# Expert choice in 44 steps a half, all 32 gate groups beside up tiles 95 to 126, and ScalarE's up program as straight code

## What is computed

```python
q = (h @ peer_q).reshape(B, S, 8, 2, 128)
scores = jnp.einsum('bshpd,hpkd->bshpk', q, peer_keys)      # 128 keys each
s, i = lax.top_k(scores, 16)
cand_s = s[..., 0, :, None] + s[..., 1, None, :]            # 256 a head
cand_i = i[..., 0, :, None] * 128 + i[..., 1, None, :]
top_s, sel = lax.top_k(cand_s, 16)
idx = jnp.take_along_axis(cand_i, sel, axis=-1)             # of 16384 experts
gate = jax.nn.softmax(top_s, axis=-1)
act = gelu(einsum('td,ted->te', h, peer_u[idx]))            # exact Gelu
out = einsum('te,ted->td', gate * act, peer_v[idx])
```

## Time and profile before

| What | us |
|---|---|
| runs: median of 3 (lowest, highest) | 4202.78 (4199.14, 4202.87) |
| the profiled execution, its own time | 4196.4 |
| its span, first to last instruction | 4194.6 |
| TensorE matmul busy in the span | 4031.4 |
| VectorE busy | 3057.9 |
| ScalarE busy | 2412.3 |
| GpSimd busy | 434.2 |

### The profile page before, as it was taken

How to read it: one execution, slowest core, us unless ns; L and a number is a source line. 1 busy time by engine, 2 the same in 40 slices (tenths; PEclk the granted TensorE clock), 3 DMA queues, 4 the chain that set the end, 5 groups by cost and what they waited for, 6 DMA issues and landing times.

```text
span 4194.6 us, 82991 instructions
## 1 busy us (share of the span) xinstructions
PE 4031.4 (96%) x30146; PEld 3719.3 (89%) x30146; DVE 3057.9 (73%) x4990; ACT 2412.3 (58%) x4061; POOL 434.2 (10%) x442
## 2 busy tenths in 40 slices
PE   6899999999999999999998999999998999999999
PEld 6899999788899999978888999988887799998887
DVE  6758879767565786986766678788775578787555
ACT  4246668544533665854556566774444466686544
POOL 0000015100000000520000000441000000052000
PEclk9999999999999999999998999999998899999999
DMA  8345442778513445367853445338883244533554
GB/s 292 108 137 178 177 172 100 246 245 289 174 48 136 168 177 180 111 211 249 284 179 106 179 175 180 143 126 298 283 288 111 82 166 178 180 131 116 193 192 155
DMA packets 203667, 749.27 MB, mean 179 GB/s; under 512 B 22704, under 2 KB 23856, under 8 KB 202192
## 3 DMA queue, kind: packets, MB, share of 16 engines
q1 hardware_dynamic: 178416, 646.51, 44.1%
q0 software_dynamic: 25056, 100.15, 7.5%
HBM read 745.52 MB, written 1.05 MB: 178 GB/s over the span
## 4 chain that ended last, share of the span: by engine, by line
PE 89%; ACT 5%; DVE 4%; issue 1%; DMA 1%; SPq 0%; ACTq 0%; DVEq 0%
PE ps L1953 15%; PE ps L1954 14%; PE ps L1960 14%; PE ps L2397 11%; PE ps L2400 11%; PE ps L2404 11%; PE ps L2379 4%; PE ps L2101 2%; ACT oh L1028 1%; ACT t_hi L656 1%; ACT oh L1020 1%; PE ps L1974 1%; DMA raw<-w_tiles 1%; PE ps L2354 1%; PE ps L2245 1%
## 5 line engine op out<-in xcount | busy, mean ns | idle before, releaser
L1129 DVE TENSOR_TENSOR t_lo<-raw,t_hi 128x1024 fp32r<-128x1024 f32 x1180 | 1445.4, 1225 | 921.8 <-ACT t_hi L656 902.3
L656 ACT CAST t_hi<-raw 128x1024 fp32r<-128x1024 f32 x1180 | 1239.5, 1051 | 1429.7 <-PE ps L2404 700.4
L1953 PE MATMUL ps<-h_hi,t_hi 128*128 128x256 f32 x5344 | 1353.3, 290 | 44.4 <-DVE h_lo L1261 20.2
L1954 PE MATMUL ps<-h_lo,t_hi 128*128 128x256 f32 x5344 | 1323.8, 285 | 0.0
L1953 PEld LDWEIGHTS ps<-h_hi,t_hi 128*128 128x128 f32 x5344 | 1031.6, 193 | 69.2 <-issue 46.0
L1954 PEld LDWEIGHTS ps<-h_lo,t_hi 128*128 128x128 f32 x5344 | 1034.8, 194 | 0.7 <-issue 0.5
L1960 PE MATMUL ps<-h_hi,t_lo 128*128 128x256 f32 x5240 | 735.1, 283 | 0.0
L1960 PEld LDWEIGHTS ps<-h_hi,t_lo 128*128 128x128 f32 x5240 | 676.1, 192 | 0.0
L2397 PE MATMUL ps<-t_hi,h_hi 128*128 128x512 f32 x2048 | 549.9, 390 | 11.6 <-DVE h_lo L1844 11.6
L2400 PE MATMUL ps<-t_hi,h_lo 128*128 128x512 f32 x2048 | 549.9, 390 | 0.0
L2404 PE MATMUL ps<-t_lo,h_hi 128*128 128x512 f32 x2048 | 548.1, 389 | 0.0
(11 more groups left out here) (291 smaller groups left out, 3413.1 us busy)
## 6 DMA issues: line engine op xcount, KB each, us to landing
raw<-u_tiles SPq DMA_DIRECT2D x512, 512.0 KB, 3.2
raw<-v_tiles SPq DMA_DIRECT2D x512, 512.0 KB, 4.2
raw<-w_tiles SPq DMA_DIRECT2D x188, 512.0 KB, 3.6
oh<-w_tiles POOLq DMA_DIRECT2D x160, 512.0 KB, 4.9
arena<-w_tiles SPq DMA_DIRECT2D x16, 512.0 KB, 3.6
arena<-keys_t POOLq DMA_DIRECT2D x4, 1024.0 KB, 5.1
arena<-mla_w POOLq DMA_DIRECT2D x1, 4096.0 KB, 14.4
arena<-lora POOLq DMA_DIRECT2D x2, 1280.0 KB, 8.1
```

The source lines that it names most:

```text
L656: act.copy(t_hi[:, j % SPL, :], raw[:, j % RAW, :]).then_inc(hi_done, 1)
L1129: tts(t_lo[:, j % SPL, :], raw[:, j % RAW, :], t_hi[:, j % SPL, :].bitcast(F32), ALU.subtract).then_inc(lo_done, 1)
L1953: mm(o, hi[:, c, :], h_hi[:, c, :], start=(c == 0), stop=False)
L1954: mm(o, hi[:, c, :], h_lo[:, c, :], start=False, stop=False)
```

## The change

The choice gets 44 steps a half: each pair of heads takes three steps (18 to 29) where it took four. The gates begin at tile LATE = 2 x 44 + 7 = 95, so all 32 groups stand beside tiles 95 to 126, with tile 127 alone behind them. GpSimd fills the slots from 95 on. The one-hot rows stay in one buffer. VectorE makes the columns and rows of group 0 behind its subtractions of tiles 92 and 93, and takes the first down tile's subtraction beside group 31, and tile 127's product last. ScalarE's part for the up tiles is a plain Python loop, so the instructions stand in a row with no branch; Exp runs between the cast and the Gelu of its tile, its table is asked for after the Gelu before, and the two passes of group 0 stand behind one Gelu each.

```diff
--- before.py
+++ after.py
@@ -131,8 +131,9 @@
 AT_TAIL, IN_NORM = 2, [0, 2, 2, 4]
 FOLDS_BEFORE = [0, 0, 48, 96, 160]
 
-RANK_KEYS, PAIRS, RANK_PAIRS, SOFT, LOOK_UP, CHOSEN = 0, 16, 18, 34, 35, 47
-STEPS = 48
+RANK_KEYS, PAIRS, RANK_PAIRS, SOFT, LOOK_UP, CHOSEN = 0, 16, 18, 30, 31, 43
+STEPS = 44
+LATE = TT * STEPS + 7
 SMALL = {"mix0": 64, "mix1": 128, "mix2": 144, "mix3": 176}
 NORMS_BEFORE = {"out0": 1, "out1": 3, "lout": 6, "wo": 8}
 HSPLIT = {"ffn0": 3, "ffn1": 6, "ffn2": 9, "ffn3": 13, "wo": 11}
@@ -337,9 +338,7 @@
         TK_SLOT = (KEYS - -(-sum(int(np.prod(shape)) for _, shape in choice) // T)) // EB * EB
         SC_SLOT = TK_SLOT - TT * 16 * P // T
 
-        assert SC_SLOT > STEPS + PAIRS + 2 and TK_SLOT > TT * STEPS + 6
-        BOTH = KEYS - TK_SLOT
-        assert BOTH < GROUPS and BOTH % 2 == 0
+        assert SC_SLOT > STEPS + PAIRS + 2 and TK_SLOT > LATE > SC_SLOT + 2 and (LATE + 1) % EB == 0 and KEYS - LATE == GROUPS + 1
         tk = carve([("w", (DC, T)), ("keys", (16, P)), ("q", (16, T)), ("gap", (SC_SLOT * T - 8192,)),
                     ("sc", (TT, 16, P)), *choice])
         sum_sb = carve([("gap", (24 * D,)), ("sum", (TT, D))])["sum"]
@@ -381,9 +380,7 @@
         wa_hi, wa_lo = h_hi, h_lo
         def hot_rows(l, m):
 
-            if m < BOTH or m % 2 == 0:
-                return acc[:, :].rearrange("p (q k) -> p q k", q=8)
-            return t_lo[:, (SEGS[f"u{l}"][0] + 1) % SPL, :].rearrange("p (q k) -> p q k", q=8)
+            return acc[:, :].rearrange("p (q k) -> p q k", q=8)
 
         hot_cols = [v[:, :, :, :].rearrange("p a q k -> p (a q) k") for v in (oh1, oh2)]
 
@@ -599,7 +596,8 @@
 
                 n = T // 8
                 pool.wait_ge(sel_ready, TT * (l + 1))
-                pool.memset(arena[:, TK_SLOT * T:KEYS * T], 1.0).then_inc(ones_in, 1)
+                pool.memset(act_slot(LATE, None), 1.0)
+                pool.memset(arena[:, (LATE + 1) * T:KEYS * T], 1.0).then_inc(ones_in, 1)
                 for m in range(n):
                     if m >= 2:
                         pool.wait_ge(gates_t, n * l + m - 1)
@@ -1033,20 +1031,19 @@
 
                 name = f"u{l}"
                 first = SEGS[name][0]
-                distances(l, 0)
-                weights(l, 0)
-                for k in range(TK_SLOT, KEYS):
+                below = SEGS[f"v{l}"][0]
+                for k in range(LATE, KEYS):
                     b = (first + k) % 2
                     if k + 2 < KEYS:
                         upper(first + k + 2, first + k + 2, None, name)
+                    elif k + 2 == KEYS:
+                        upper(below, below, None, f"v{l}")
                     else:
                         act.wait_ge(tile_used, first + k + 1)
                     act.activation(ps[:, b, 0:T], ps[:, b, 0:T], ACT.Gelu).then_inc(act_up, 1)
-                    distances(l, k - TK_SLOT + 1)
-                    weights(l, k - TK_SLOT + 1)
-                for m in range(BOTH + 1, GROUPS):
-                    distances(l, m)
-                    weights(l, m)
+                    if k - LATE + 1 < GROUPS:
+                        distances(l, k - LATE + 1)
+                        weights(l, k - LATE + 1)
 
             def peer(l):
                 project(f"q{l}", lambda k, b: act.copy(tk["q"][:, at(k), :], ps[:, b:b + 1, 0:T]), f"u{l}")
@@ -1061,23 +1058,23 @@
                 def gelu(k, i, b):
                     act.activation(act_slot(k, i), by_quads(ps[:, b, 0:T]), ACT.Gelu).then_inc(taken, 1)
 
-                def step(n, j, k, i):
-                    upper(n, j, i, name)
-                    gelu(j - first - 2, i, j % 2)
-                a = 2
-                for tt in range(TT):
-                    b = STEPS * tt + SOFT + 3
-                    in_loops(act, name, a, b, step)
-                    a = b
-                    seen(sm_in)
-                    act.activation(tk["e"][:, 2], tk["e"][:, 2], ACT.Exp).then_inc(sm_exp, 1)
-                in_loops(act, name, a, SC_SLOT + 2, step)
-                seen(ranked)
-                in_loops(act, name, SC_SLOT + 2, TK_SLOT + 2, step)
+                for k in range(2, LATE + 2):
+                    upper(first + k, first + k, None, name)
+                    if k in (SOFT + 3, STEPS + SOFT + 3):
+                        seen(sm_in)
+                        act.activation(tk["e"][:, 2], tk["e"][:, 2], ACT.Exp).then_inc(sm_exp, 1)
+                    if k == SC_SLOT + 2:
+                        seen(ranked)
+                    gelu(k - 2, None, (first + k) % 2)
+                    if k in (SOFT + 2, STEPS + SOFT + 2):
+                        act.preload_act_table(ACT.Exp)
+                    if k == LATE - 1:
+                        distances(l, 0)
+                    elif k == LATE:
+                        weights(l, 0)
                 tiles_and_hots(l)
                 name = f"v{l}"
                 first = SEGS[name][0]
-                upper(first, first, None, name)
                 act.wait_ge(gated, GROUPS * (l + 1))
 
                 def upper_gated(k, i, j):
@@ -1752,9 +1749,17 @@
                                 link(cp(idf, idx))
                             link(pair_sums(k - PAIRS))
                         elif k < SOFT:
-                            h, second = divmod(k - RANK_PAIRS, 2)
-                            link(next8(tk["c2"], cs[:, h, :], ci[:, h, :]) if second
-                                 else first8(tk["cand"][:, h, :], tk["c2"], cs[:, h, :], ci[:, h, :]))
+                            h, third = 2 * ((k - RANK_PAIRS) // 3), (k - RANK_PAIRS) % 3
+                            other = tk["cand"][:, h + 1, :]
+                            if third == 0:
+                                link(first8(tk["cand"][:, h, :], tk["c2"], cs[:, h, :], ci[:, h, :]))
+                            elif third == 1:
+                                next8(tk["c2"], cs[:, h, :], ci[:, h, :])
+                                link(dve.max(cs[:, h + 1, 0:8], other))
+                                dve.max_index(ci[:, h + 1, 0:8], cs[:, h + 1, 0:8], other)
+                            else:
+                                link(dve.match_replace(tk["c2"], cs[:, h + 1, 0:8], other, LOWEST))
+                                link(next8(tk["c2"], cs[:, h + 1, :], ci[:, h + 1, :]))
                         elif k == SOFT:
 
                             tts(e[:, 2], cs, cs[:, :, 0:1].broadcast_to([P, HEADS, TOPK]), ALU.subtract)\
@@ -1775,7 +1780,6 @@
                 for k in range(a, a + 4):
                     lower(first + k, first + k, name)
                 sel_out(1)
-                in_loops(dve, name, a + 4, TK_SLOT + 2, lambda n, j, k, i: lower(n, j, name))
 
             def gates(l):
 
@@ -1799,40 +1803,41 @@
                 def activated(k):
 
                     b = (first + k) % 2
-                    dve.wait_ge(act_up, BOTH * l + k - TK_SLOT + 1)
-                    dve.wait_ge(gated, GROUPS * l + k - TK_SLOT)
+                    dve.wait_ge(act_up, (KEYS - LATE) * l + k - LATE + 1)
+                    dve.wait_ge(gated, GROUPS * l + k - LATE)
                     tts(act_slot(k, None), by_quads(ps[:, b, 0:T]), act_slot(k, None), ALU.mult).then_inc(taken, 1)
 
                 def gate(m):
 
                     dve.wait_ge(gates_t, GROUPS * l + m + 1)
-                    dve.wait_ge(taken, TAKEN[name] + min(TK_SLOT + m + 1, KEYS))
+                    dve.wait_ge(taken, TAKEN[name] + LATE + m + 1)
                     view = act_quads[:, :, 2 * m:2 * m + 2, :].rearrange("p b q x -> p q b x")
                     bank = GATE_BANKS[m % 2]
                     tts(view, ps[:, bank:bank + 2, :].rearrange("p q (b x) -> p q b x", x=4 * EB),
                         view, ALU.mult).then_inc(gated, 1)
 
-                dve.wait_ge(sel_ready, TT * (l + 1))
-                columns(0)
-                rows(0)
+                for k in range(TT * STEPS + 4, LATE + 2):
+                    lower(first + k, first + k, name)
+                    if k == TT * STEPS + 4:
+                        dve.wait_ge(sel_ready, TT * (l + 1))
+                        columns(0)
+                    elif k == TT * STEPS + 5:
+                        rows(0)
                 dve.wait_ge(ones_in, l + 1)
-                for k in range(TK_SLOT, KEYS):
-                    m = k - TK_SLOT
-                    columns(m + 1)
+                for k in range(LATE, KEYS - 1):
+                    m = k - LATE
+                    if m + 1 < GROUPS:
+                        columns(m + 1)
                     if k + 2 < KEYS:
                         lower(first + k + 2, first + k + 2, name)
+                    else:
+                        lower(SEGS[f"v{l}"][0], SEGS[f"v{l}"][0], f"v{l}")
                     activated(k)
                     dve.wait_ge(gates_t, GROUPS * l + m + 1)
-                    rows(m + 1)
+                    if m + 1 < GROUPS:
+                        rows(m + 1)
```

(18 more changed lines are left out.)

## The result

The changed kernel takes 4136.31 us (median of 4 runs, 4135.73 to 4141.58) against 4200.96 (4 runs, 4198.74 to 4202.87): a ratio of 0.9849, 95% interval 0.9832 to 0.9866, 64.7 us less. The forecast was 4133.0, with a range of 4122 to 4150. In a later set of five rounds it was 4135.04 against 4199.03, ratio 0.9845 (0.9831 to 0.9858).

A forecast was written before the change was run, and what follows sets the result against it. TensorE, 89% of the span, was taken as the bound, so only its idle or late time counts. Savings of 4 x (12.0 + 4.2) plus 4.6 for the clock, 69.4 us, gave 4133 us, range 4122 to 4150.

The forecast's parts named there:

- Part 1: Gates moved to tiles 95 to 126, with 1.5 us idle before the down tiles: 12.0 us a layer saved.
- GpSimd's fill: Fill of the slots, grown to 8448 columns: 7.2 us, done in tile 93, before group 0 asks; cover about 4 us.
- its lead of 2.3 us: VectorE's subtractions in the up tiles run 2.3 us ahead of TensorE's need, covering middle steps of 3.05 us.
- Part 2: The choice in 44 steps a half: costed at nothing; moves 0.33 us of transposes from one stretch to the other.
- Part 3: ScalarE's up tiles written out without loops: tiles 0 to 94 take 275.5 us, 4.2 us a layer saved.
- The clock, 4.6 us: TensorE's clock stays granted after the idle before the down tiles: 4.6 us saved over layers 0 to 2.
- the stretch at 69%: Eight gate groups without a tile, TensorE busy 20.78 of 30.00 us, taken as partly behind the clock's falls.
- The clock did not fall: Rival: the clock still falls after 1.5 us idle before the down tiles, giving 4137.6 us; chance 0.22.
- The Exp tiles are not dear: Rival: eight Exp tiles stay dear, 1.15 us more each, giving 4142 us; chance 0.06.
- The loads did go: Rival: table loads stay with the Gelus or the early load buys a second reload, 4150 us; chance 0.06.
- Neither helper became the bound: Rival: VectorE or ScalarE becomes the bound beside the gates, 4146 us and up; chance 0.06.
- ScalarE's straight code is delivered in time: Rival: delivery of ScalarE's straight up-tile code stalls it, about 4228 us at 0.25 us a tile; chance 0.03.

The follow-up runs named there:

- the first experiment: Only the choice's 44 steps a half put into the kernel before, gates still from tile 104 and ScalarE still in loops: 4212.54 us.
- the longer seam: Changed kernel plus a table load and small copy on ScalarE between the last Gelu and the first gated block: 4137.60 us.
- the gates back at 104: Changed kernel with its gates from tile 104 and eight groups without a tile, keeping 44 steps and ScalarE's straight code: 4176.79 us.

## Why the prediction was right, and the one term it missed

The gain was forecast as 69.4 us and is 64.7 between the medians. That the time itself is off by 3.3 us only, 4136.3 for 4133.0, is in part luck: the median of the kernel before came out 1.8 us lower with one more run.

- **Part 1, 12.0 us a layer.** Right to the tenth: 165.42 - 153.39 = 12.03. The pace of 4.657 us, group 0 without a wait and a seam of 1.5 us were the working, and each shows in the rows above (the idle of 1.34 us is that seam less the modelled end of the last matmul). The first group's 1.17 us are gone.
- **GpSimd's fill.** Its length was right (0.31 + 6.93 for 7.2), and group 0 did not wait for it. What the prediction looked at was only who waits for the fill. The step that failed stands in part 1: that the operations are the same ones in the same order, with 0 for group 0's work in its new place. VectorE's columns of group 0 stand in no term of the sum; they were moved under the fill, and there they take 5.19 us for 0.59. That ate the 1.1 us that VectorE would have idled there, its lead of 2.3 us, which I had named as the cover of the middle steps, and 1.06 us more. It cost 1.27 us a layer, 5.1 in all, and is the whole difference between 69.4 and the 65.0 us measured, but for 0.3 at the clock and 0.4 in layer 0. Moving the columns and cutting the fill both give it back.
- **Part 2, nothing.** Right: the middle step takes 2.87 us, where 3.05 were worked out, so it never drew on the lead. What was missed is a side of it that the change itself takes away, the second Exp at a loop's entry, so it touched only the first experiment.
- **Part 3, 4.2 us a layer.** Right in size: 275.5 us were forecast for tiles 0 to 94 and 275.5 measured where the fill does not meet the columns. The sum was right with half of the loads unseen: each loop turn had a second one, ahead of the cast. In the turn of the earlier trace rows it ended at 331.25, 0.25 us before the cast could start (331.50, behind TensorE), so it cost nothing there. Kept were one load at the first Gelu and 0.48 us at each Exp (0.38 and the 0.10 of the next tile), where 0.5 was said.
- **The clock, 4.6 us.** Right, 4.9, but half of the reason was wrong. I held the stretch at 69% ahead of the hole partly to blame; the longer seam shows the same falls without it. Why one seam in four is spared stays open.
- **The rivals.** The clock did not fall behind a hole of 1.34 us. The Exp tiles are not dear (3.26 us), but only by the early request (4.68 without it). The loads did go. Neither helper became the bound. ScalarE's straight code is delivered in time: its tiles come 2.88 us apart.

## What to carry to other kernels

When an instruction moves, ask not only who waits for it and what it waits for, but which instruction of GpSimd runs at its new place: a long fill there can hold a short instruction of VectorE to its end, and all that is queued behind it. Where two operations must overlap, cut the long one in pieces or put the short one behind it. And a lead is one budget: name all that draws on it before costing a move at nothing.

## What was not expected of the hardware

- **A fill of GpSimd holds VectorE's column instruction, but not its subtraction.** 128 columns from one fp32 tensor in SBUF, 0.34 us alone, ended only with the fill, 5.13 us after its start for the first column and 4.94 for the second; a subtraction of 1024 columns with two inputs in SBUF took 1.23 us inside the same fill, as it does alone. The Trainium skill (GPSIMD Engine Reference, Specifications) says that GpSimd's interfaces to SBUF are shared with VectorE, with contention for instructions in a two-port mode or with two inputs in SBUF. For the columns the trace agrees, if that is the mode they run in, which no run here shows; the Trainium skill (VectorE: DVE Perf Modes, Mode 2×_2P) gives such a mode to instructions with one tensor input in SBUF, in fp32 too, and not to those with two. The subtraction was not held beside this fill, which only writes. Beside GpSimd's columns, which also read, the next two subtractions took 1.31 and 1.32 us for 1.23, and GpSimd's own second and third column 1.39 and 1.41 us, where its shortest take 0.79.
- **The hold is by the instruction.** With fills of 0.95 us the two columns took 0.93 and 0.74 us, though the fills followed without a gap.
- **The clock behind a hole.** In the 13 executions read, counting the two profiled ones of before and after and leaving out the one at 0.65, 36 seams had a hole of 1.05 or 1.34 us and none was followed by a fall to 1.2 GHz; 16 had one of 2.90 to 2.93 us and 12 were. Which of the four is spared differs: layer 3 in the kernel before and in the longer seam, layer 0 with the 44 steps, layer 1 with the gates back at 104. A fall costs 1.6 us (2.9 in the one, with the 44 steps, that lasted twice as long). The execution at 0.65 is not like the others in this: three of its four seams of 1.34 us were followed by a granted clock of 0.50 for 3.4 us. That the same hole may or may not be answered fits the Trainium skill's free-running monitor (TensorE: Matmul & The Clock Gate, Part 1).
- **One execution ran at a granted clock of 0.65 from about 47 us on, with falls to 0.50.** Its cause is open; the same kernel did not do it again.
